# Narrow expert rounds in a two-layer transformer kernel: unsplit fp32 weights in two column tiles in place of high and low halves

## The chip, the cores and the metric

One core of one Trainium2 chip runs the whole program. The metric is the device time of one execution in microseconds, given as the median of three runs.

## The reference

Two blocks follow one another on x of 256 tokens by 1024 features, in float32. The first block has two layers; the second of them ends in a mixture of experts, and that is the part in question. The second block (attention over compressed and selected keys, retention, convolution, a 4096-wide feed-forward part) is untouched.

```
def moe_ffn(x, router_w, w1, w3, w2):
    logits = (xt @ router_w).astype(F32)
    top_v, top_i = lax.top_k(logits, TOP_K)                 # 2 of 8 experts for each token
    top_w = jax.nn.softmax(top_v, axis=-1)
    gates = jnp.sum(jax.nn.one_hot(top_i, N_EXPERTS) * top_w[..., None], axis=1)
    for e in range(N_EXPERTS):
        y = y + gates[:, e:e + 1] * swiglu(xt, w1[e], w3[e], w2[e])
# swiglu(x, w1, w3, w2) = (silu(x @ w1) * (x @ w3)) @ w2 ; w1, w3: 1024 x 3584, w2: 3584 x 1024
```

## The kernel before, in words

**Units.** All weights come through one ring of slots, loaded by SyncE in the order of use. In the expert part a unit is 128 x 2048 floats (1 MB). One expert takes 42 units: 28 for w1 and w3 (front units, `first_unit`), 14 for w2 (back units, `back_unit`). The ring has 9 slots there; `unit` on SyncE loads into a slot once TensorE has finished with the unit that held it.

**Halves.** A weight is used as two fp32r numbers: ScalarE writes the high half of a unit (`ahead`, L2049), VectorE the low half (`split`, L2660: weight minus high half), three units ahead of TensorE. A dense product is then three fp32r matmuls (`products`, L1081 to L1083: high x high, high x low, low x high), so a dense unit is 12 matmuls with 512 moving columns.

**Rounds.** Experts are sorted by their number of tokens. Eight rounds run: rounds 0, 2, 4, 6 are dense (up to 128 tokens), rounds 1, 3, 5, 7 are few (`few(r)`, up to 64 tokens). Round 2 (`LARGE`) holds up to 32 tokens beyond 128; these "thin" tokens use the unsplit weights in plain fp32, four column tiles of 32 at a time (`thin_tiles`, L1620). Further rounds stand under a condition and don't run with this input.

**A few round.** Its 64 token columns lie in the array twice, high half beside low half of the activations (`gathered_few`, 128 columns). `products_few` (L1612, L1613) multiplies these by the high and by the low weights: a few unit is 8 matmuls of 512 columns. The result has high and low contributions in different PSUM rows, so ScalarE copies it out raw (`raw_out`, L2260), TensorE turns and adds it by a matmul with a folding matrix (`turn_tile`, L1581, 8 matmuls for a 512-wide tile), ScalarE applies silu (L2288), VectorE multiplies (L3240) and the product is split in halves again (L2304, L3260). Round 3 uses transposes (L1599) and sums on VectorE (L3247) in place of the folding matmuls.

**Order.** The order is written out by hand. Step s runs the front of round s, and in between the back of round s-1 (`first_matrices`, `back_after`): two front units, one back unit. Step 0 has no back, step 8 is the back of round 7 alone (`second_matrix`). After set unit numbers come the small pieces: transposes (`turned_after`), gathers of tokens for the next round (L1503), gate rows (L1540, L1543) and scattering of the finished round (L1555, in two pieces `add_spare` on VectorE, L3226). Each engine walks the same list and waits by semaphores.

Of the kernel before, what the change touches and what calls it, by code (L numbers as in the profile page):

```python
# [52 lines left out]
EXPERT_LEAD = EXPERT_HIGHS - 1  # L53
# [143 lines left out]
class Counts:  # L197


    def __init__(self):  # L200
# [4 lines left out]
        self.raws, self.folded, self.few_turned = Tally(), Tally(), Tally()  # L205
# [21 lines left out]
ADDED_CHOOSE_AT, ADDED_GATHER_AT = 11, (13, 14, 15, 16, 20, 21, 22, 23)  # L227
# [37 lines left out]
def thin(lot):  # L265

    return lot[1] == THIN


def gather_order(r):  # L270


    return (0, 2, 4, 6, 1, 3, 5, 7) if any(map(thin, gathered_lots(r))) else tuple(range(8))


def bank_lots(r, i):


    return [lot for lot in gathered_lots(r) if i == 0 or not thin(lot)]
# [22 lines left out]
def outputs_before(r):  # L302

    return 2 * r + (1 if r > LARGE else 0)


def few_before(r):

    return sum(few(q) for q in range(r))
# [19 lines left out]

def large_units():  # L330


    stream = [unit for s in range(N_EXP + 1) for unit in step_units(s)]
    at = [n for n, (r, _) in enumerate(stream) if r == LARGE]
    assert [stream[n][1] for n in at] == list(range(MOE_UNITS))
    return at
# [16 lines left out]
def first_place(r, i):  # L353
# [4 lines left out]
    if i < PAIRED:  # L358
        pair, at = divmod(i, 2 * PAIR_UNITS)
        m, k = divmod(at, PAIR_UNITS)  # L360
        banks = [0, 1] if r == LARGE + 1 else [2 * m, 2 * m + 1]
        return [2 * pair, 2 * pair + 1], m, k, banks
    m, k = divmod(i - PAIRED, TILE_UNITS)
    return [LAST_TILE], m, k, [m if r in (LARGE - 1, LARGE + 1) else 2 * m]
# [12 lines left out]
def turned_after(r, i):  # L377
# [3 lines left out]
    if r == LARGE + 1:  # L381
        return []
    return [i // 4 - 2, i // 4 - 1] if i >= 9 and i % 8 == 1 else []


def adds_up(r):

    return r in (LARGE, LARGE + 1)


def added_after(r, i):

    if r == LARGE:
        return [i // 4] if i % 4 == 2 else []
    return [i // 4 - 2 + i % 8 - 1] if r == LARGE + 1 and i >= 9 and i % 8 in (1, 2) else []


def lows_after(r, i):

    if i < 2 or not few(r):  # L400
        return []
    if not adds_up(r):
        return turned_after(r, i - 2)
    return added_after(r, i - 2) + (added_after(r, i - 1) if i == FIRST_UNITS - 1 else [])


def gather_at(r):

    return LARGE_GATHER_AT if r == LARGE else ADDED_GATHER_AT if adds_up(r) else GATHER_AT


def choose_at(r):

    return LARGE_CHOOSE_AT if r == LARGE else ADDED_CHOOSE_AT if adds_up(r) else CHOOSE_AT + (2 if r == 0 else 0)


def tail_added_at(r):

    return TAIL_AT if r == LARGE + 1 else None


def tail_low_at(r):

    if r is None or not few(r):
        return None
    return TAIL_AT + 2


def rounds(eng, body, routed, extra, ids=False):
# [21 lines left out]
    further(0)  # L451

# [7 lines left out]
def build(nc, A, out):  # L460
    ctx = ExitStack()
    with ctx:
# [74 lines left out]
        with one:  # L537
# [31 lines left out]
            fold = sb("fold", [P, FEW], where=one)  # L569
# [9 lines left out]
        gathered_few = [params_parts[:, i * 1024:(i + 1) * 1024].rearrange("p (c n) -> p c n", n=P)  # L579
                        for i in range(2)]  # L580

        def gathered(lot):

            _, _, _, many, place = lot
            if thin(lot):
                return [thin_x]
            return gathered_many if many else [gathered_few[place][:, :, i * FEW:(i + 1) * FEW] for i in range(2)]
# [7 lines left out]
        def pairs_of(bank):  # L595

            return bank[:, :].rearrange("p (k n c) -> p k c n", c=EXPERT_ROWS, n=P)
# [8 lines left out]
        ye_high, ye_low = gparts[:, 1024:2048], gparts[:, 2048:3072]  # L606
# [6 lines left out]
        raw_few = [gbuf[:, a:a + 1024].rearrange("p (i n) -> p i n", i=2) for a in (0, 2048)]  # L613
# [15 lines left out]
        def raw_of(r, t, m):  # L629

            return thin_raw[m] if r == LARGE else raw_few[m][:, t % 2, :]

# [3140 lines left out]
```

## Time and profile before

| | us |
|---|---|
| median of 3 runs | 2295.61 (2289.98 to 2296.39) |
| the profiled execution's own time | 2291.09 |
| its span | 2289.1 |
| TensorE busy | 2240.2 (98%) |
| VectorE busy | 1821.1 (80%) |
| ScalarE busy | 1377.9 (60%) |
| mean granted TensorE clock | 0.998 |
| moved from HBM | 580 MB, 254 GB/s over the span |

The expert part lies between 428.3 and 1383 us. Busy time of TensorE counts a matmul from its start to the end of its latency, so matmuls that follow each other at 0.23 us show 0.39 us each; the pace is read from start to start. PE is TensorE's multiplication, PEld its weight load, DVE VectorE, ACT ScalarE, SP or SPq SyncE and its DMA queue. In the timeline the second number of a merged row is the time from the first start to the last end.

### The profile page before, as it was taken

The numbers are of one execution on the slowest core, as the hardware profiler recorded it, in microseconds if no ns is written. First come the engines' busy times: TensorE is split into PE (matmuls) and PEld (weight loads), VectorE is DVE, ScalarE is ACT, GpSimd is POOL, SyncE is SP. The second block draws the span as 40 slices with busy tenths as digits, with TensorE's granted clock in tenths as the row PEclk, the third lists the DMA queues.
The fourth block names the chain that finished last, engine by engine and source line by source line (L and its number), as shares of the span: only waits on it lengthen the run. The fifth ranks groups of instructions, "written<-read, shape, count | busy, mean of one in ns | idle before, by whom it ended". The sixth has DMA issues, their size and how long they took to land.

```text
span 2289.1 us, 29232 instructions
## 1 busy us (share of the span) xinstructions
PE 2240.2 (98%) x11083; PEld 1818.3 (79%) x11083; DVE 1821.1 (80%) x2362; ACT 1377.9 (60%) x1569; POOL 31.7 (1%) x44
## 2 busy tenths in 40 slices
PE   8999998999999999999999998999999999999998
PEld 6788887888866677788887876888888888888887
DVE  4965468989878898999899997999764579987555
ACT  4444444578756777787878883565454436654543
POOL 0000000000000000000000000000000000000000
PEclk9999999999999999999999999999999999999999
DMA  8366554699978999999999996545566665355563
GB/s 289 111 214 189 185 166 166 261 338 408 363 257 294 328 366 350 367 408 414 397 384 407 413 381 213 165 125 164 167 203 193 182 191 173 112 190 179 188 189 120
DMA packets 198507, 584.19 MB, mean 255 GB/s; under 512 B 17259, under 2 KB 26615, under 8 KB 183640
## 3 DMA queue, kind: packets, MB, share of 16 engines
q1 hardware_dynamic: 196060, 573.97, 71.1%
q0 software_dynamic: 1872, 6.82, 0.8%
q8 instruction: 91, 1.49, 0.3%
q10 hardware_dynamic: 428, 1.45, 0.2%
q14 instruction: 56, 0.46, 0.1%
HBM read 580.07 MB, written 2.12 MB: 254 GB/s over the span
## 4 chain that ended last, share of the span: by engine, by line
PE 85%; DVE 9%; ACT 2%; issue 2%; DMA 1%; POOL 0%; DVEq 0%; POOLq 0%; ACTq 0%; SPq 0%
PE tile L1081 20%; PE tile L1083 19%; PE tile L1082 19%; PE aux L1204 3%; DVE units_parts L2660 3%; PE tile L1612 3%; PE tile L1613 3%; PE aux L1081 2%; PE tile L1620 2%; PE aux L1083 2%; PE aux L1082 2%; PE aux L1613 1%; PE aux L1612 1%; PE aux L1581 1%; PE aux L1503 1%
## 5 line engine op out<-in xcount | busy, mean ns | idle before, releaser
L2660 DVE TENSOR_TENSOR units_parts<-units,high 128x1024 fp32r<-128x1024 f32 (+3 forms) x339 | 482.4, 1441 | 87.5 <-ACT high L2049 84.6
L1082 PE MATMUL tile<-units_parts,acts 128*128 128x512 f32 (+2 forms) x1344 | 513.7, 382 | 0.0
L2049 ACT ACTIVATE high<-units 128x1024 fp32r<-128x1024 f32 (+3 forms) x339 | 412.3, 1235 | 150.1 <-PE tile L1083 44.3
L1081 PE MATMUL tile<-high,acts 128*128 128x512 f32 (+2 forms) x1012 | 401.4, 397 | 8.2 <-DVE units_parts L2660 3.4
L1083 PE MATMUL tile<-high,acts 128*128 128x512 f32 (+2 forms) x1012 | 388.8, 384 | 0.0
L1082 PEld LDWEIGHTS tile<-units_parts,acts 128*128 128x128 f32 x1344 | 253.1, 188 | 46.5 <-issue 1.7
L1081 PEld LDWEIGHTS tile<-high,acts 128*128 128x128 f32 x1012 | 190.4, 188 | 56.8 <-issue 17.7
L1083 PEld LDWEIGHTS tile<-high,acts 128*128 128x128 f32 x1012 | 190.1, 188 | 38.5
L1082 PE MATMUL tile<-units_parts,zbuf_parts 128*128 128x512 f32 x328 | 127.6, 389 | 0.0
L1083 PE MATMUL tile<-high,zbuf_parts 128*128 128x512 f32 x256 | 99.7, 389 | 0.0
L3411 DVE SCALAR_TENSOR_TENSOR zbuf<-cbuf,taps,zbuf 128x256 f32<-128x256 f32 x240 | 99.6, 479 | 0.0
L2660 DVE TENSOR_TENSOR units_parts<-units,acts 128x2048 fp32r<-128x2048 f32 x39 | 89.2, 2287 | 12.8 <-ACT acts L2049 12.6
L2080 ACT ACTIVATE acts<-aux 128x512 fp32r<-128x512 f32 x48 | 27.3, 596 | 117.5 <-PE aux L1204 117.4
L2660 DVE TENSOR_TENSOR units_parts<-units,gbuf_parts 128x2048 fp32r<-128x2048 f32 x39 | 89.1, 2285 | 7.0 <-ACT gbuf_parts L2049 6.9
L1612 PE MATMUL tile<-high,params_parts 128*128 128x512 f32 x220 | 87.4, 397 | 1.9 <-ACT gbuf L2260 1.9
L1613 PE MATMUL tile<-units_parts,params_parts 128*128 128x512 f32 x224 | 87.5, 391 | 0.0
L2049 ACT ACTIVATE gbuf_parts<-units 128x2048 fp32r<-128x2048 f32 x39 | 74.8, 1919 | 12.3 <-PE tile L1083 8.1
L2049 ACT ACTIVATE acts<-units 128x2048 fp32r<-128x2048 f32 x39 | 74.7, 1915 | 4.2 <-PE tile L1083 2.3
L1081 PE MATMUL tile<-high,zbuf_parts 128*128 128x512 f32 x184 | 72.2, 392 | 0.0
L3699 DVE TENSOR_TENSOR gbuf<-gbuf 128x1024 f32<-128x1024 f32 x16 | 19.6, 1226 | 66.1 <-ACT gbuf L2073 66.1
L2073 ACT ACTIVATE gbuf<-tile,row_scale 128x512 f32<-128x512 f32 x36 | 24.3, 687 | 79.4 <-PE tile L1083 79.3
L1082 PEld LDWEIGHTS tile<-units_parts,zbuf_parts 128*128 128x128 f32 x328 | 61.6, 188 | 12.4
(567 smaller groups left out, 5067.6 us busy)
## 6 DMA issues: line engine op xcount, KB each, us to landing
units<-in_moe_w SPq DMA_DIRECT2D x156, 1024.0 KB, 7.9
units<-in_w_in SPq DMA_DIRECT2D x134, 512.0 KB, 4.0
units<-in_w_ff SPq DMA_DIRECT2D x128, 512.0 KB, 3.7
q_buf<-in_moe_w SPq DMA_DIRECT2D x39, 1024.0 KB, 7.6
k_buf<-in_moe_w SPq DMA_DIRECT2D x39, 1024.0 KB, 7.7
nat<-in_moe_w SPq DMA_DIRECT2D x39, 1024.0 KB, 8.0
bias<-in_moe_w SPq DMA_DIRECT2D x39, 1024.0 KB, 8.6
units<-in_ffn_w SPq DMA_DIRECT2D x48, 512.0 KB, 4.2
```

What stands on the lines that cost most here:

```text
L1081: nc.tensor.matmul(bank, lhs[0], high, start=start, stop=False)
L1082: nc.tensor.matmul(bank, lhs[0], low, start=False, stop=False)
L1083: return nc.tensor.matmul(bank, lhs[1], high, start=False, stop=stop)
L1204: mm = nc.tensor.transpose(bank[0:m, i * k:(i + 1) * k], src, ident[0:k, 0:k])
L1612: nc.tensor.matmul(bank[:, :], both, high, start=start, stop=False)
L1613: return nc.tensor.matmul(bank[:, :], both, low, start=False, stop=stop)
L1620: mm = nc.tensor.matmul(bank[at, :], rows_, of, start=start, stop=stop, tile_position=(0, c * THIN))
L2049: nc.scalar.activation(high_slot(SG[0], n) if wide_ else high_slot(SG[0], n)[:, 0:cols], halves(weights) if wide_ else weights[:, 0:cols], ...
L2073: nc.scalar.activation(dst, tiles[n % 4][:, 0:width], func, scale=scale).then_inc(SG[0].tile_evac, 1)
L2080: nc.scalar.activation(dst, aux[k % 4][0:p, 0:n * m].rearrange("p (n m) -> p n m", n=n), ACT.Copy).then_inc(SG[0].turned_high, 1)
L2660: V.tensor_tensor(low, weights, high, ALU.subtract).then_inc(SG[0].low_ready, 1)
L3411: ins = V.scalar_tensor_tensor(y_t[:, c, :], u_t[:, c, j:j + SEQ], taps[:, c, j:j + 1], y_t[:, c, :], ALU.mult, ALU.add)
```

## The change

In rounds with at most 64 tokens the weights are no longer split. `raw_unit` waits for the load alone; `few_tiles` multiplies the 64 token columns by the unsplit weights in plain fp32, output columns 0 to 511 in array columns 0 to 63, output columns 512 to 1023 in array columns 64 to 127. A few unit becomes 4 such matmuls of 512 columns (8 of 256 in the last tile). Both halves of the output lie in one PSUM bank, silu and product are taken there as in a dense round, and 4 transposes turn two 512-wide tiles; the folding matmuls, the raw copies and the second splitting go, in round 3 too. ScalarE and VectorE pass over the few rounds' units (`splits`), and look up to 4 units ahead (`led_to`). Gathers for a few round fetch whole tokens (high and rest added in the bank) instead of two halves. The few rounds' scattering takes 64 rows of the array at a time.

```
+def split_units():
+    return [n for n, (r, _) in enumerate(EXPERT_STREAM) if not few(r)]
...
+        def led_to(sig_, n):
+            m = expert_unit(sig_, n)
+            own = [of for of in split_at if of > m][:EXPERT_LEAD]
+            return n + max([1] + [of - m for of in own if of - m <= UNIT_LEAD])
...
+                    def raw_unit():
+                        n = C.unit.take()
+                        weights, _, loaded, loads = slot(S, n)
+                        pe.wait_ge(loaded, 16 * loads)
+                        return weights
+
+                    def few_tiles(bank, width, lhs, weights, start, stop):
+                        for h in range(2):
+                            mm = nc.tensor.matmul(bank[h * FEW:(h + 1) * FEW, 0:width], lhs,
+                                                  weights[:, h * width:(h + 1) * width], start=start, stop=stop,
+                                                  tile_position=(0, h * FEW))
+                        return mm
...
-                                if few(r):
-                                    mm = products_few(tiles[bank], both[:, at_k, :], high[:, row_, at], low[:, row_, at],
-                                                      start, stop)
...
+                        if few(r):
+                            width = 512 if paired else 256
+                            weights = raw_unit().rearrange("p (c n) -> p c n", c=chunks)
+                            for c in range(chunks):
+                                at_k = chunks * k + c
+                                mm = few_tiles(tiles[banks[0]], width, gathered(lots(r)[0])[0][:, at_k, :],
+                                               weights[:, c, :], at_k == 0, at_k == KC - 1)
...
-                        if few(r) and not adds_up(r):
-                            raws_of(r, t)
-                            bank = spare_bank("folded", r, t)
-                            for m in range(2):
-                                for c in range(4):
-                                    at = m * 4 * FEW + c * FEW
-                                    mm = nc.tensor.matmul(bank[:, at:at + FEW], raw_of(r, t, m)[:, c * P:(c + 1) * P],
-                                                          fold[:, :], start=True, stop=True)
...
                         if few(r):
-                            parts = [(sel_t, ye_high), (sel_t, ye_low)]
+                            rows_ = slice(h * FEW, (h + 1) * FEW)
+                            nc.tensor.matmul(bank[:, :], sel_t[rows_, b, :], ye_high[rows_, :], start=True, stop=False,
+                                             tile_position=(h * FEW, 0))
...
@@ ScalarE (ahead) and VectorE (split) @@
                     n = C.split.take()
+                    if not splits(SG[0], n):
+                        continue
...
@@ SyncE (multiplied), after the last round @@
-                sp.wait_ge(ye_ready, outputs_before(r + 1) - 1)
+                sp.wait_ge(ye_ready, outputs_before(r + 1))
```

In the instruction order a row is an operation with output and inputs, its size (output rows by moving columns for a matmul), and how often it stands in a row. The first place is TensorE in step 5 (front of round 5, back of round 4), where the first two tiles of round 5 are turned. Before:

```order
L1083 MATMUL aux1<-gbuf_parts,zbuf_parts 128x512
L1612 MATMUL tile0<-high,params_parts 128x512
L1613 MATMUL tile0<-units_parts,params_parts 128x512
L1612 MATMUL tile0<-high,params_parts 128x512
L1613 MATMUL tile0<-units_parts,params_parts 128x512
L1612 MATMUL tile1<-high,params_parts 128x512
L1613 MATMUL tile1<-units_parts,params_parts 128x512
L1612 MATMUL tile1<-high,params_parts 128x512
L1613 MATMUL tile1<-units_parts,params_parts 128x512
L1581 MATMUL aux3<-fold,gbuf 128x64 x8
L1581 MATMUL aux2<-fold,gbuf 128x64 x8
```

With the change, at the same place (L1599 is `few_tiles`, L1566 the transposes, L1073 to L1075 the dense product):

```order
L1075 MATMUL aux1<-acts,zbuf_parts 128x512
L1599 MATMUL tile0<-units,params 64x512 x4
L1566 MATMUL aux2<-consts_sb,gbuf 128x128 x4
L1599 MATMUL tile0<-units,params 64x512 x4
L1073 MATMUL aux0<-gbuf_parts,zbuf_parts 128x512
L1074 MATMUL aux0<-bias2_parts,zbuf_parts 128x512
L1075 MATMUL aux0<-gbuf_parts,zbuf_parts 128x512
```

A few unit is one group of 4, the 16 folding matmuls are 4 transposes, and the array goes from full width to 64-column tiles and back twice within these rows. The second place is TensorE in step 3 with the change, near its end, where full-width gathers (L1495, L1501), few units and thin groups (L1609, four tiles of 32 columns) meet:

```order
L1501 MATMUL aux2<-sc_parts,x_sb_parts 128x64 x2
L1599 MATMUL tile1<-nat,params 64x512 x4
L1495 MATMUL aux3<-sc_parts,x_sb_parts 128x128 x4
L1609 MATMUL tile2<-bias2,gain 32x512 x4
L1599 MATMUL tile1<-units,params 64x512 x4
L1073 MATMUL aux0<-high,zbuf_parts 128x512
```

Here the tile width changes from 32 to 64 directly, with no full-width work between. The third place is VectorE in step 5, whose low halves (L2660 before, L2624 after) dense units wait for. Before:

```order
L2660 TENSOR_TENSOR units_parts<-units,acts 128x2048
L2660 TENSOR_TENSOR units_parts<-units,gbuf_parts 128x2048
L2660 TENSOR_TENSOR units_parts<-units,high 128x2048 x2
L2660 TENSOR_TENSOR bias2_parts<-bias2,acts 128x2048
L2660 TENSOR_TENSOR q_buf_parts<-q_buf,gbuf_parts 128x2048
L3240 TENSOR_TENSOR zbuf<-zbuf,aux3 128x4x64
L3240 TENSOR_TENSOR zbuf<-zbuf,aux2 128x4x64
L2660 TENSOR_TENSOR k_buf_parts<-k_buf,high 128x2048
L2660 TENSOR_TENSOR nat_parts<-nat,high 128x2048
L2660 TENSOR_TENSOR gain_parts<-gain,acts 128x2048
L3260 TENSOR_TENSOR zbuf_parts<-zbuf,zbuf_parts 128x4x64 x2
```

With the change (L3189 adds scattered rows, L3222 multiplies silu by the second product, L3154 chooses tokens):

```order
L3189 TENSOR_TENSOR acc<-acc,aux3 128x512
L3189 TENSOR_TENSOR acc<-acc,aux2 128x512
L2624 TENSOR_TENSOR units_parts<-units,acts 128x2048
L3222 TENSOR_TENSOR gbuf<-gbuf,tile1 128x512
L2624 TENSOR_TENSOR bias2_parts<-bias2,gbuf_parts 128x2048
L2624 TENSOR_TENSOR nat_parts<-nat,high 128x2048
L2624 TENSOR_TENSOR units_parts<-units,high 128x2048
L3154 TENSOR_SCALAR sc_parts<-consts_sb,by_round 128x128 x4
```

Only the dense back units are split now; the ring's other slots go by unsplit.

## Rows read from the trace of the kernel before

**Rows 1.** Windows of steps 0 to 8: start:end, length, busy per engine, clock, DMA share, GB/s

```profile
428.30:513.10 84.80, 83.68 (x402) 69.83 (x401) 77.37 (x62) 63.07 (x53) 0.00 (x0) 1.00 0.93 341
513.10:624.50 111.40, 110.96 (x572) 90.77 (x571) 99.85 (x59) 92.95 (x85) 0.00 (x0) 1.00 1.00 390
624.50:780.20 155.70, 152.38 (x806) 104.87 (x804) 121.04 (x116) 98.37 (x93) 0.00 (x0) 1.00 0.82 285
780.20:902.40 122.20, 117.67 (x595) 85.41 (x595) 108.92 (x76) 90.20 (x85) 0.00 (x0) 1.00 0.98 360
902.40:1015.50 113.10, 113.10 (x502) 91.06 (x503) 106.52 (x65) 89.81 (x66) 0.00 (x0) 1.00 0.97 376
1015.50:1125.90 110.40, 108.39 (x540) 89.96 (x539) 102.81 (x65) 92.99 (x88) 0.00 (x0) 1.00 1.03 411
1125.90:1236.20 110.30, 110.30 (x504) 90.47 (x503) 104.11 (x63) 87.54 (x64) 0.00 (x0) 1.00 1.01 389
1236.20:1340.00 103.80, 102.16 (x496) 84.03 (x495) 97.66 (x59) 85.87 (x69) 1.64 (x3) 1.00 1.03 411
1340.00:1383.00 43.00, 38.97 (x163) 28.45 (x162) 37.04 (x26) 28.80 (x22) 0.00 (x0) 1.00 0.75 305
```

**Rows 2.** What the DMA queue itself waited for, 428.3 to 1383: total us, times, longest

```profile
SPq L878 <- PE tile L1083: 341.9, 110, 18.9
SPq L878 <- PE tile L1613: 232.3, 116, 5.0
```

**Rows 3.** DMA issues of expert weights: count, KB each, median us from issue to landing

```profile
units<-in_moe_w SPq DMA_DIRECT2D x156, 1024.0 KB, 7.9
```

**Rows 4.** Groups by line, VectorE, 428.3 to 1383: busy, mean ns, idle before and releaser

```profile
L2660 DVE TENSOR_TENSOR units_parts<-units,high 128x2048 fp32r<-128x2048 f32 x78 | 177.3, 2287 | 25.2 <-ACT high L2049 24.9
```

**Rows 5.** Timeline of TensorE, a few unit of round 5 and the folding behind it

```profile
1078.67 0.39 PE L1612 MATMUL tile<-high,params_parts 128*128 128x512 f32 x1
...
1080.26 0.39 PE L1613 MATMUL tile<-q_buf_parts,params_parts 128*128 128x512 f32 x1
1080.49 1.78 PE L1581 MATMUL aux<-fold,gbuf 128*128 128x64 f32 x15
```

**Rows 6.** Pool means in the first block, two tiles of 64 columns: timeline, then the line's durations

```profile
84.39 1.08 PE L1384 MATMUL aux<-zbuf 128*64 128x256 f32 x8
...
L1384 PE MATMUL aux<-zbuf x32: 379/379/431, 84.4 to 379.4; 128*64 128x256 f32 x32
```

**Rows 7.** Full-width plain fp32 of 512 columns (scattering): timeline, then the line's durations

```profile
1355.06 1.88 PE L1555 MATMUL aux<-gbuf,zbuf 128*128 128x512 f32 x4
...
L1555 PE MATMUL aux<-gbuf,zbuf x32: 590/592/667, 638.7 to 1362.4; 128*128 128x512 f32 x32
```

**Rows 8.** Timeline of TensorE around one thin group, full width before and behind it

```profile
642.79 0.49 PE L1599 MATMUL aux<-consts_sb,zbuf 128*128 128x128 f32 x3
643.21 1.06 PE L1620 MATMUL tile<-units,params 128*32 128x512 f32 x8
644.21 0.50 PE L1081 MATMUL tile<-high,acts 128*128 128x512 f32 x1
644.54 0.40 PE L1082 MATMUL tile<-units_parts,acts 128*128 128x512 f32 x1
```

**Rows 9.** Groups by line, the folding matmuls: count, busy, mean ns

```profile
L1581 PE MATMUL aux<-fold,gbuf 128*128 128x64 f32 x336 | 38.8, 273 | 0.0
```

**Rows 10.** Waits of TensorE, 428.3 to 1383: total us, times, longest

```profile
PE tile L1612 <- DVE units_parts L2660: 3.1, 8, 1.0
PE tile L1081 <- ACT gbuf L2260: 2.6, 1, 2.6
PE tile L1612 <- ACT gbuf L2260: 1.9, 2, 1.0
PE tile L1612 <- DVE gbuf L3273: 1.8, 1, 1.8
...
PE aux L1081 <- DVE bias_parts L2660: 1.2, 1, 1.2
```

More of the change, by code:

```diff
@@ L262, in lots, with unsplit @@
     return [(2 * FEW, CAP, column_of(r), True, 0)] + ([(4 * FEW, THIN, ROUNDS, False, 1)] if r == LARGE else [])
-def thin(lot):
-    return lot[1] == THIN
+def unsplit(lot):
+    return not lot[3]
 def gather_order(r):
-    return (0, 2, 4, 6, 1, 3, 5, 7) if any(map(thin, gathered_lots(r))) else tuple(range(8))
+    return (0, 2, 4, 6) if all(map(unsplit, gathered_lots(r))) else (0, 2, 4, 6, 1, 3, 5, 7)
 def bank_lots(r, i):
-    return [lot for lot in gathered_lots(r) if i == 0 or not thin(lot)]
+    return [lot for lot in gathered_lots(r) if i == 0 or not unsplit(lot)]
 def gathered_lots(r):
@@ L302, in outputs_before @@
 def outputs_before(r):
-    return 2 * r + (1 if r > LARGE else 0)
-def few_before(r):
-    return sum(few(q) for q in range(r))
+    return sum(1 if few(q) else 3 if q == LARGE else 2 for q in range(r))
 def column_of(r):
@@ L451, in rounds @@
     further(0)
+EXPERT_STREAM = [unit for s in range(N_EXP + 1) for unit in step_units(s)]
 def wait(eng, sem, value):
@@ L1498, in gather_bank @@
                         width = columns.stop - columns.start
[L1499 removed]
+                        both = [slice(lot[0], lot[0] + lot[1]) for lot in lots_ if unsplit(lot)]
                         for i in range(2):
@@ L1508, in gather_bank @@
                                 for b in range(TB):
-                                    mm = nc.tensor.matmul(bank[:, first:first + THIN], rest[:, b, at],
+                                    mm = nc.tensor.matmul(bank[:, first:first + own.stop - own.start], rest[:, b, at],
                                                           chosen[:, b, own], start=False, stop=(b == TB - 1))
@@ L1700, in back_unit @@
                         if k == 0:
-                            for h in range(2):
+                            for h in range(1 if few(r) else 2):
                                 take_bank(out_bank(r, h), ye_ready, out_first + h + 1)
@@ L1711, in back_unit @@
                                 chunk = EXPERT_ROWS * k + c
[L1712 to L1719 removed]
+                                mm = products(aux[h][:, :], [part[:, chunk, :] for part in hide_t],
+                                              high[:, c, at], low[:, c, at], chunk == 0, chunk == D_FFE // P - 1)
+                            if k == BACK_UNITS - 1 and h == 0:
                                 mm.then_inc(S.tile_full, 1)
@@ L2059, in used @@
                 C.unit.take(units)
-                if expert_unit(SG[0], C.unit.n - 1) >= 0:
-                    lead = EXPERT_LEAD
-                ahead(min(C.unit.n + lead, END[0]))
+                last = C.unit.n - 1
+                ahead(min(led_to(SG[0], last) + 1 if expert_unit(SG[0], last) >= 0 else C.unit.n + lead, END[0]))
             def evac(dst, closes, func=ACT.Copy, width=512, scale=1.0, also=None, units=None):
@@ L2306, in tiles_out @@
                     def tiles_out(r, i):
                         tiles_, m, _, banks = first_place(r, i)
-                        if m == 1 and not few(r):
+                        if m == 1:
                             return
@@ L3284, in first_matrices @@
                     tiles_, m, _, banks = first_place(r, i)
-                    if closes(r, i) and m == 1 and not few(r):
+                    if closes(r, i) and m == 1:
                         dve.wait_ge(S.unit_done, C.unit.n)
```

337 lines of the change are left out of this document (130 added, 207 removed).

## The prediction

> **What bounds the kernel now.** I read the windows of the expert part first, step by step, since the change touches nothing else [rows 1]. They add up to 954.7 us of the 2289. TensorE is in flight for 937.6 us of them, VectorE for 855, and HBM delivers up to 411 GB/s: three resources near their limit, so the question is which of them the steps wait for. The DMA queue's own waits settle it for the loads: SyncE stood 574 us behind TensorE alone in the two rows shown [rows 2]. It issues a load when TensorE frees a slot of the nine, and a load lands 7.9 us later [rows 3], about three units' time. So some five or six units lie landed ahead of TensorE. The weights follow TensorE, they don't lead it, although at 411 GB/s a unit of 1.049 MB costs 2.55 us and a step of 42 units 107 us, little less than steps 4 to 6 take. VectorE needs 2.29 us for each low half [rows 4], 96 us for a step of 42, and has its other work beside; TensorE waits for it and for ScalarE's copies in places, some 11 us in the larger entries [rows 10]. The path is mostly TensorE's own issue, so I price the change on TensorE, and then ask what VectorE and the loads do.
>
> **The passes.** A few unit is 8 fp32r matmuls. From the first to the last start of one are 1.59 us for 7 steps, 0.227 each [rows 5], so 1.82 us a unit, and 4 rounds of 42 units are 168. With the change it is 4 plain fp32 matmuls of 512 columns, two on either half of the array. Plain fp32 shows two records per matmul, 0.43 us apart at 512 columns ((1.88 - 0.59) / 3, [rows 7]). Whether two tiles of 64 columns run side by side is visible already: four such fp32 matmuls of 256 columns give eight records, whose first starts spread over 1.08 - 0.38 = 0.70 us [rows 6]. One after another they would spread over 7 x 0.215 = 1.5; as pairs over 3 x 0.215 = 0.65. So they pair, and a unit is four steps of 0.43, 1.72 us. 168 x (1.82 - 1.72) = **16 us less**; if the step is 0.455, nothing.
>
> **The folding.** 336 records at 0.108 apart ((1.78 - 0.27) / 14, [rows 5, 9]) go: **36 us less**. Fourteen transposes for each few round come, 56 in all at 0.11, 6 us; round 3 loses as many of its own (L1599, 7 tiles of 8). These cancel.
>
> **The edges.** The array's tile width changes between full-width and column-tiled work, and a weight load isn't pulled over such a change. The thin groups show the price. The last of three transposes starts at 642.79 + 0.49 - 0.27 = 643.01; the thin group starts at 643.21, where 643.12 would be the pace: 0.09. From there to the second dense matmul at 644.54 are 1.33 us, where two passes and one fp32r matmul make 1.09: 0.24. Together 0.33 us for one excursion [rows 8]. Before, 42 thin groups each make one. Counting in the changed order every stretch that isn't full-width, I find 23, 24, 18, 14, 21, 14, 18 and 4 in steps 1 to 8, 136 in all. 94 more at 0.33: **31 us more**. Inside these stretches 50 changes between tiles of 32 and 64 columns, or to the 64-row scattering, have no row; they lie between nothing and a full 0.33, and I take 0.15, near the 0.09 of an entry: **7.5 us more** (0 to 16).
>
> What drains at an edge is stated by the Trainium skill (TensorEngine Tiling (Array Packing), Key Properties): a change of tiling mode, not of tile alone, drains TensorE. That rule speaks against a kernel that changes modes 136 times; it names no price, the 0.33 us above is this trace's.
>
> **Gathers, scattering, end.** Round 1, 3, 5 and 7's tokens are gathered whole: 128 matmuls and 80 narrow ones in place of 160 and 16, about **2 us more** at 0.11. Few scattering keeps its count. The next block's loads now wait for all of the last output rather than its first half: **0.7 us more**, ScalarE's copy being one instead of two in turn.
>
> **Waits.** VectorE loses 168 low halves of 2.29 us, ScalarE as many high halves; VectorE falls to about half busy in the few steps. The waits on low halves and on raw copies in rows 10 (3.1, 2.6, 1.9, 1.8, 1.2) make 10.6 us, and step 8 goes at VectorE's pace (37.0 of 43.0 us busy) where TensorE needs about 3 less: **14 us less** (0 to 17). For these I name no new wait: silu and product of a few tile have the 6 us of the next units, as in dense rounds.
>
> **Sum.** -16 - 36 + 31 + 7.5 + 2 + 0.7 - 14 = -25 us, against the profiled execution's own 2291.1: 2266. The median of the runs is 4.5 above that execution, the runs spread over 6.4. I put the median after at **2267**.
>
> **Do the loads keep up?** By the same terms steps 4, 6 stay near 112, step 5 falls to 104 and step 7 to about 96. Five landed units are worth 13 us. Step 5 needs 3 of them, gets them back in step 6, step 7 needs 11, and step 8 has 14 units (36 us) for its 36. It holds, narrowly.
>
> **Rivals.**
> - *The waits stay* (12%). Other late work takes the place of the low halves, such as products that stand behind unit_done. Then only TensorE's own terms count: 2267 + 12 = 2279. For it: the few steps have closing waits in both forms. Against: VectorE is half idle.
> - *The loads become the bound* (6%). If the landed units are fewer than I think, steps 5 and 7 take 107 each: 3 + 11 us more, 2281. For it: 411 GB/s at a share of 1.03 in these steps [rows 1]. Against: the queue waits for TensorE [rows 2].
> - *Edges cost more than they give* (5%), the case on the slower side. All 144 edges added (94 + 50) stand against 61 us of gain elsewhere, so from 0.43 us each there is none. At 0.55, if a 64-column tile loads its weights later than a 32-column one or the drain of a row-tiled group is longer, 79 us stand against 61: 2311. Against: the entry into the pool means is no longer than into a thin group.
> - *Column tiles overlap only in part* (2%). Then a unit has more than four steps: at, say, 1.6 times one tile's pace in place of 2 it would be 8 x 0.43 / 1.6 = 2.15 us, and 168 x 0.43 = 72 us more, 2339. The spread of 0.70 us [rows 6] speaks against it, and so does the thin group with four tiles in 1.06 us [rows 8]. The Trainium skill (TensorE: Matmul & The Clock Gate, Measured speedup vs the span model) gives 2.38x for three column tiles, which would be such a case; the rows here don't bear it out.
>
> That the change doesn't do what it says has no room: the changed order has no folding and 168 low halves fewer.
>
> **The numbers.** The forecast case has 75%, with a range of its own from 2250 to 2278. Below it: inner changes free and edges at the 0.18 of two entries alone, 21 us less, 2246. Above: waits stay and the step is 0.44 instead of 0.43 (7 us), 2286. The range 2247 to 2286 takes these in and leaves out the two slow rivals and some of the rest. A measurement here can tell 0.3%, 7 us, from no change: below 2288.7 is faster. The forecast, the first two rivals and little else lie there: 0.89; 0.05 within, 0.06 slower.
>
> **What would show it.** Few units at 1.72 us on TensorE, with steps of 0.43; dense ones unchanged. Excursions at 0.33. L2660's successor with 168 fewer, its waits gone from TensorE's list. Steps 1, 3, 5, 7, 8 shorter by 4 to 8 us each, 4 and 6 unchanged within 2, 2 shorter by about 2. Wrong would be: steps 5 and 7 at 107 with TensorE waiting for `in_moe_w`; step 4 or 6 longer by over 4; a spacing of 0.86 between a tile's records.

## The result and the profile after

| | before | after |
|---|---|---|
| median of the runs, us | 2296.4 | 2274.4 |
| range of the runs, us | 2290.0 to 2302.7 | 2270.7 to 2280.2 |
| profiled execution, own time / span, us | 2291.1 / 2289.1 | 2274.4 / 2272.6 |
| expert part, steps 0 to 8, us | 949.8 | 930.6 |

The ratio is 0.991 with a 95% interval of 0.9883 to 0.9937: faster by 0.9%, inside the range, 7 us less gain than the forecast of 2267. Of the 16.7 us between the two profiled executions the expert part holds 19.2; the start of the part lies 2.2 later, behind work that the change does not touch.

Windows of the steps after the change, answering to [rows 1] (start:end, length, then busy time of PE, PEld, DVE, ACT and POOL, the granted clock as a share, the DMA share and GB/s):

```profile
430.50:515.40 84.90, 83.87 (x403) 69.65 (x401) 74.60 (x59) 58.61 (x47) 0.00 (x0) 1.00 0.92 338
515.40:626.40 111.00, 107.98 (x527) 56.94 (x526) 41.33 (x26) 40.34 (x42) 0.00 (x0) 0.97 1.00 394
626.40:776.60 150.20, 150.05 (x786) 87.66 (x784) 85.52 (x95) 65.58 (x68) 0.00 (x0) 1.00 0.83 288
776.60:893.60 117.00, 116.31 (x608) 58.03 (x605) 44.20 (x32) 40.88 (x42) 0.00 (x0) 1.00 0.99 377
893.60:1009.90 116.30, 116.30 (x497) 75.11 (x497) 69.41 (x44) 57.45 (x43) 0.00 (x0) 1.00 0.98 384
1009.90:1112.70 102.80, 102.80 (x505) 56.01 (x501) 43.03 (x31) 39.52 (x40) 0.00 (x0) 1.00 1.02 410
1112.70:1225.80 113.10, 113.10 (x491) 73.67 (x492) 70.81 (x44) 57.51 (x44) 0.00 (x0) 1.00 1.01 403
1225.80:1331.90 106.10, 98.55 (x456) 50.63 (x452) 37.14 (x24) 30.95 (x25) 1.64 (x3) 0.99 1.02 412
1331.90:1361.10 29.20, 29.12 (x123) 9.32 (x122) 2.75 (x4) 1.10 (x3) 0.00 (x0) 0.99 0.85 355
```

Steps 2, 3 and 5 are shorter by 5.5, 5.2 and 7.6 us. Step 1 gained 0.4 where 4 to 8 was forecast, steps 4 and 6 are longer by 3.2 and 2.8. The boundary between steps 7 and 8 is drawn a little differently here; together they took 141.9 (to the last unit at 1378.1) and take 135.3, 6.6 less where 8 to 16 was forecast. VectorE went from 109 busy to 44 in step 3, so it is no limit any more. In steps 1 and 7, PE is busy 3 and 7.5 us less than the step is long, and in step 1 the clock's mean is 0.97: those two steps have waits.

TensorE's own time, from the spacing of the matmul starts over all steps, each start charged at its form's pace. What lies up to 0.25 us above the pace is called an edge, what lies above that a wait:

| us | dense | few | thin | fold, transposes, gathers, scatter | edges | waits |
|---|---|---|---|---|---|---|
| before | 456.6 | 304.2 | 36.0 | 111.1 | 21.3 | 20.2 |
| after | 456.6 | 288.0 | 36.0 | 77.0 | 53.6 | 18.6 |
| difference | 0 | -16.2 | 0 | -34.1 | +32.3 | -1.6 |

The first four columns are counts times pace. Passes that ran at half clock, described below, are in the last two columns: some 3 us of them count as edges and some 2 as waits. The few units and the folding went as forecast. Edges grew by less than the 38.5 forecast; waits hardly fell. The timeline of TensorE in step 5 shows two few units with transposes between them and a dense unit on either side (start, length, engine, line, operands, count):

```profile
1040.71 0.39 PE L1075 MATMUL aux<-acts,zbuf_parts 128*128 128x512 f32 x1
1041.03 1.94 PE L1599 MATMUL tile<-units,params 128*64 128x512 f32 x8
1042.90 0.66 PE L1566 MATMUL aux<-consts_sb,gbuf 128*128 128x128 f32 x4
1043.49 1.94 PE L1599 MATMUL tile<-units,params 128*64 128x512 f32 x8
1045.36 0.50 PE L1073 MATMUL aux<-gbuf_parts,zbuf_parts 128*128 128x512 f32 x1
1045.69 0.40 PE L1074 MATMUL aux<-bias_parts,zbuf_parts 128*128 128x512 f32 x1
1045.93 0.39 PE L1075 MATMUL aux<-gbuf_parts,zbuf_parts 128*128 128x512 f32 x1
```

A few unit is eight records, two at a time. From 1043.49 to 1045.36 are 1.87 us: four steps of 0.43 and 0.15 for the first pair and the way out. The way in is 0.09 (0.32 from the last dense start to the first few start, where 0.227 is the pace), and the first dense matmul behind takes 0.33 instead of 0.227, another 0.10. Some 0.34 us for an excursion, and the next few dense passes stand at 0.23 to 0.24: the thin group of [rows 8] again, for a few unit.

What TensorE waited for, 430 to 1362 (us in total, times, longest), answering to [rows 10]:

```profile
PE aux L1073 <- DVE k_buf_parts L2624: 3.1, 1, 3.1
PE tile L1609 <- DMA bias<-in_moe_w: 3.0, 1, 3.0
PE aux L1073 <- DVE bias_parts L2624: 2.3, 2, 1.6
PE aux L1073 <- DVE units_parts L2624: 1.1, 1, 1.1
PE aux L1073 <- DVE nat_parts L2624: 1.1, 1, 1.1
PE aux L1495 <- DVE zbuf_parts L3197: 1.0, 1, 1.0
```

The waits for low halves (L2624, the L2660 of before) are there again, but they are others: each belongs to one of the last five dense units of step 7, and the halves are late because the load was. ScalarE (ACT), which makes the high half, waited for that load, and VectorE (DVE) followed ScalarE, here for the fourth of the five:

```profile
1315.25 1.91 ACT L2037 ACTIVATE high<-bias 128x2048 fp32r<-128x2048 f32 x1 [6.90 <-DMA bias<-in_moe_w]
1317.20 2.29 DVE L2624 TENSOR_TENSOR bias_parts<-bias,high 128x2048 fp32r<-128x2048 f32 x1 [5.93 <-ACT high L2037]
1319.63 0.47 PE L1073 MATMUL aux<-high,zbuf_parts 128*128 128x512 f32 x1 [1.55 <-DVE bias_parts L2624]
```

From the landing to the first matmul are 4.4 us, the time that the two halves take one behind the other.

The two places, in TensorE's timeline. The end of step 1:

```profile
604.00 1.95 PE L1599 MATMUL tile<-nat,params 128*64 128x256 f32 x16
605.87 0.66 PE L1566 MATMUL aux<-consts_sb,gbuf 128*128 128x128 f32 x4
609.55 1.93 PE L1609 MATMUL tile<-bias,params 128*32 128x512 f32 x8 [3.02 <-DMA bias<-in_moe_w]
611.41 3.68 PE L1599 MATMUL tile<-units,params 128*64 128x256 f32 x16
615.02 1.31 PE L1609 MATMUL tile<-q_buf,params 128*32 128x512 f32 x8
```

The thin group of round 2 waits 3.0 us for its load. Behind the wait everything is slow: the group itself takes 1.93 instead of 1.06 [rows 8], and the sixteen records of 256 columns take 3.68 where the same form took 1.95 at 604.00. That is the lower of the clock's two levels, 1.2 in place of 2.4 GHz: the granted clock is 0.50 from 608.7 to 615.6. From start to start the group takes 0.87 us more than at full clock, the unit 1.74, the next group 0.24: 2.9 us behind a wait of 3.0. The end of step 7:

```profile
1322.56 1.95 PE L1599 MATMUL tile<-q_buf,params 128*64 128x256 f32 x16
1327.62 0.50 PE L1073 MATMUL aux<-acts,zbuf_parts 128*128 128x512 f32 x1 [3.11 <-DVE k_buf_parts L2624]
...
1329.23 0.63 PE L1073 MATMUL aux<-acts,zbuf_parts 128*128 128x512 f32 x1
1329.66 0.63 PE L1074 MATMUL aux<-k_buf_parts,zbuf_parts 128*128 128x512 f32 x1
```

A wait of 3.1 us for the last dense unit, and 1.6 us into that unit the passes fall to 0.43 apart, half pace, some 1.6 us lost. Neither stretch is in the profile of before.

### The profile page after: what moved, and what is told of

Its sections match the earlier page's. It is cut to its first block, busy times and chain, and to the rows that moved or that the text cites. A ratio compares the mean times of both kernels' runs of the same rounds, so it can differ in the third digit from the quotient of the medians.

```text
span 2272.6 us, 28182 instructions
## 1 busy us (share of the span) xinstructions
PE 2225.7 (98%) x10907; PEld 1623.4 (71%) x10907; DVE 1435.7 (63%) x2135; ACT 1041.6 (46%) x1301; POOL 31.7 (1%) x44
## 4 chain that ended last, share of the span: by engine, by line
PE 92%; DVE 4%; DMA 2%; issue 1%; ACT 0%; SPq 0%; POOL 0%; POOLq 0%; ACTq 0%; DVEq 0%
PE tile L1073 21%; PE tile L1075 20%; PE tile L1074 20%; PE tile L1599 9%; PE aux L1196 3%; PE aux L1599 3%; PE aux L1073 2%; PE aux L1074 2%; PE aux L1075 2%; PE tile L1609 2%; PE aux L1907 1%; DMA k_buf<-in_moe_w 1%; PE aux L1495 1%; PE aux L1566 1%; PE aux L1550 1%
## 5 line engine op out<-in xcount | busy, mean ns | idle before, releaser
L2624 DVE TENSOR_TENSOR units_parts<-units,high 128x1024 fp32r<-128x1024 f32 (+3 forms) x299 | 392.1, 1329 | 134.7 <-ACT high L2037 129.9
L2037 ACT ACTIVATE high<-units 128x1024 fp32r<-128x1024 f32 (+3 forms) x299 | 336.2, 1145 | 167.3 <-DMA units<-in_w_in 40.0
L1073 PE MATMUL tile<-high,acts 128*128 128x512 f32 (+2 forms) x1012 | 404.9, 400 | 6.0 <-DVE units_parts L2624 3.4
L1075 PE MATMUL tile<-high,acts 128*128 128x512 f32 (+2 forms) x1012 | 390.5, 386 | 0.0
L1073 PEld LDWEIGHTS tile<-high,acts 128*128 128x128 f32 x1012 | 191.3, 189 | 61.9 <-issue 18.2
L1075 PEld LDWEIGHTS tile<-high,acts 128*128 128x128 f32 x1012 | 190.9, 189 | 39.3
L1599 PE MATMUL tile<-units,params 128*64 128x512 f32 (+1 forms) x520 | 108.7, 550 | 0.0
L1075 PE MATMUL tile<-high,zbuf_parts 128*128 128x512 f32 x256 | 99.7, 389 | 0.0
L2067 ACT ACTIVATE acts<-aux 128x512 fp32r<-128x512 f32 x48 | 27.4, 598 | 117.0 <-PE aux L1196 117.0
L1073 PE MATMUL tile<-high,zbuf_parts 128*128 128x512 f32 x184 | 72.2, 392 | 0.0
L1599 PEld LDWEIGHTS tile<-units,params 128*64 128x64 f32 x520 | 34.0, 139 | 52.4 <-issue 48.4
L1074 PEld LDWEIGHTS tile<-units_parts,zbuf_parts 128*128 128x128 f32 x328 | 61.6, 188 | 12.4
L2624 DVE TENSOR_TENSOR units_parts<-units,gbuf_parts 128x2048 fp32r<-128x2048 f32 x21 | 48.1, 2291 | 26.7 <-ACT gbuf_parts L2037 26.7
L2624 DVE TENSOR_TENSOR units_parts<-units,q_buf_parts 128x1024 fp32r<-128x1024 f32 x43 | 51.7, 1222 | 15.8 <-ACT q_buf_parts L2037 15.5
L2037 ACT ACTIVATE q_buf_parts<-units 128x1024 fp32r<-128x1024 f32 x43 | 44.8, 1062 | 33.2 <-DMA units<-in_w_ff 22.2
L2680 DVE SCALAR_TENSOR_TENSOR x_sb<-x_sb,tile 128x512 f32<-128x512 f32 x40 | 27.1, 685 | 49.7 <-PE tile L1075 49.5
```

The costliest lines, as they stand in the source:

```text
L1073: nc.tensor.matmul(bank, lhs[0], high, start=start, stop=False)
L1074: nc.tensor.matmul(bank, lhs[0], low, start=False, stop=False)
L1075: return nc.tensor.matmul(bank, lhs[1], high, start=False, stop=stop)
L1599: mm = nc.tensor.matmul(bank[h * FEW:(h + 1) * FEW, 0:width], lhs, weights[:, h * width:(h + 1) * width], start=start, stop=stop, tile_pos ...
L2037: nc.scalar.activation(high_slot(SG[0], n) if wide_ else high_slot(SG[0], n)[:, 0:cols], halves(weights) if wide_ else weights[:, 0:cols], ...
L2067: nc.scalar.activation(dst, aux[k % 4][0:p, 0:n * m].rearrange("p (n m) -> p n m", n=n), ACT.Copy).then_inc(SG[0].turned_high, 1)
```

## The experiments

Lengths in us of the steps in every kernel, from the windows of its profiled execution:

| kernel | 0 | 1 | 2 | 3 | 4 | 5 | 6 | 7+8 | all | 5 to 8 |
|---|---|---|---|---|---|---|---|---|---|---|
| before | 84.8 | 111.4 | 155.7 | 122.2 | 113.1 | 110.4 | 110.3 | 141.9 | 949.8 | 362.6 |
| changed | 84.9 | 111.0 | 150.2 | 117.0 | 116.3 | 102.8 | 113.1 | 135.3 | 930.6 | 351.2 |
| half loads | 84.8 | 105.2 | 150.2 | 116.0 | 116.3 | 102.8 | 112.9 | 125.8 | 914.0 | 341.5 |
| grouped | 84.8 | 111.3 | 148.9 | 119.1 | 113.1 | 103.6 | 109.7 | 139.3 | 929.8 | 352.6 |
| half loads, grouped | 84.8 | 103.8 | 148.8 | 116.6 | 113.2 | 101.1 | 109.8 | 123.0 | 901.1 | 333.9 |
| look-ahead 3 | 84.8 | 105.5 | 153.0 | 115.3 | 116.5 | 103.2 | 113.0 | 134.5 | 925.8 | 350.7 |
| look-ahead 3, grouped | 84.8 | 106.2 | 150.9 | 115.4 | 113.3 | 102.8 | 109.8 | 139.9 | 922.9 | 352.4 |
| early backs | 84.7 | 109.7 | 150.2 | 117.6 | 116.3 | 103.3 | 113.1 | 134.5 | 929.5 | 350.8 |
| all three | 84.7 | 107.7 | 150.8 | 115.5 | 113.2 | 102.9 | 109.8 | 138.4 | 923.0 | 351.1 |

The part before step 0 is touched by none of them, and still its end lies anywhere from 427 to 438 us in these executions. So the lengths of the steps tell apart what the medians, a few us of scatter each, can't.

**Half loads.** Few rounds load half of every unit and both column tiles multiply that half:

```diff
+                part_ = 2 if few(r) else 1
-                    unit(S, lambda v: v.rearrange("p (c n) -> p c n", c=2),
-                         w[r0:r0 + 2 * P, pair * D:(pair + 1) * D]...
+                    unit(S, lambda v: v.rearrange("p (c n) -> p c n", c=2)[:, :, 0:D // part_],
+                         w[r0:r0 + 2 * P, pair * D:pair * D + D // part_]...
...
-                                                  weights[:, h * width:(h + 1) * width], start=start, stop=stop,
+                                                  weights[:, 0:width], start=start, stop=stop,
```

> Left out: of every unit of the four few rounds only half the columns are loaded, and both column tiles multiply that half. TensorE's instructions stay the same in number, shape and order; only 168 loads carry 0.5 MB instead of 1. Theory (loads): the waits at the ends of step 1 (3.2 us) and step 7 (8.4 us) and the half clock behind them go, steps 1 and 7 are 5 and 9 us shorter, steps 4 and 6 keep their 116 and 113 within 1; the whole about 2274 - 14 = 2260. Rival (the halves' chain): ScalarE and VectorE are late there whatever has landed; under 3 us are gained, 2272. Second rival (steps 4 to 8, whose 182 units took 2.57 us each, follow the loads throughout and not only at the end): steps 4 and 6 become shorter too, over 20 us in all, below 2252.

Measured: median 2259.6, ratio to before 0.9845 (0.9819 to 0.9872). Windows of steps 1, 6, 7 and 8:

```profile
519.90:625.10 105.20, 105.20 (x528) 56.27 (x527) 41.16 (x26) 39.67 (x42) 0.00 (x0) 1.00 0.86 291
...
1110.40:1223.30 112.90, 112.90 (x489) 73.55 (x489) 69.11 (x43) 57.29 (x43) 0.00 (x0) 1.00 0.89 309
1223.30:1317.50 94.20, 94.20 (x445) 47.87 (x442) 36.83 (x24) 29.65 (x24) 1.64 (x3) 1.00 0.90 308
1317.50:1349.10 31.60, 31.60 (x134) 11.25 (x134) 3.13 (x5) 1.76 (x3) 0.00 (x0) 1.00 0.45 150
```

Step 1 is 5.8 us shorter and steps 7 and 8 together 9.5; steps 2, 4, 5 and 6 stay as they were. PE is busy the whole of every step shown, the clock is 1.00, and of the list of TensorE's waits one entry of 1.0 us remains for the whole part. By the spacing the waits are 5.4 us, 14.8 less than before the change. The 5.8 us of step 1 are its wait of 3.0 and the 2.9 at half clock. So the 14 us of waits that were to go did go, and the loads put 13 others in their place. The second rival, loads that pace steps 4 to 6 too, falls for this kernel.

**Grouped.** Second-matrix units come two at a time behind every four first-matrix units:

```diff
-        return [BACK_UNITS - 1]
-    return [i // 2 - 1] if i >= 2 and i % 2 == 0 else []
+        return [BACK_UNITS - 2, BACK_UNITS - 1]
+    return [i // 2 - 2, i // 2 - 1] if i >= 4 and i % 4 == 0 else []
```

> Second-matrix units stand in pairs behind every four first-matrix units, instead of one behind every two, in steps 1, 2 and 4 to 7. Counted in the order, TensorE leaves full width 29 times less and makes 6 fewer inner mode changes. Theory (an excursion costs 0.33 us): TensorE's edges fall from 48.6 to about 39 us; steps 4 and 6 give 1.5 us each, step 7 gives none of it (its loads are late already), the whole 2274 - 7 = 2267. Rival (the 31 us of edges are something else, such as the first matmul behind a change of operands): edges stay within 2 us of 48.6, no gain. Rival (two dense units in a row find the second one's halves late): edges fall, waits for the low halves grow by as much, no gain.

Measured: median 2271.5, ratio 0.9892 (0.9872 to 0.9913), not to be told from the changed kernel's 0.991. Edges fell by 10.7 us for 29 excursions less, 0.37 each with their inner changes, and waits grew by 10.2. Steps 4 to 8:

```profile
899.90:1013.00 113.10, 113.10 (x497) 76.26 (x497) 67.36 (x43) 54.81 (x42) 0.00 (x0) 1.00 0.99 389
1013.00:1116.60 103.60, 101.63 (x505) 56.78 (x502) 42.71 (x30) 39.79 (x40) 0.00 (x0) 1.00 1.02 410
1116.60:1226.30 109.70, 109.70 (x489) 74.74 (x489) 69.18 (x44) 56.16 (x44) 0.00 (x0) 1.00 1.03 411
1226.30:1323.60 97.30, 89.88 (x432) 46.80 (x428) 32.85 (x21) 26.97 (x21) 1.64 (x3) 1.00 1.02 411
1323.60:1365.60 42.00, 37.11 (x146) 15.66 (x146) 7.67 (x7) 6.34 (x7) 0.00 (x0) 0.92 0.87 359
```

Steps 4 and 6 gain 3.2 and 3.4 us, twice what I expected of them (the records show 7 excursions in each instead of 14, so 0.46 and 0.49 apiece, with the somewhat slower passes behind each), and steps 3, 5 and 7 with 8 give back 2.1, 0.8 and 4.0. In steps 6 and 7 HBM delivers 411 GB/s: the loads have become the pace.

**Half loads and grouped together.** The two edits above.

> Left out: half the columns of the few rounds' loads, as in the half loads run; and second-matrix units stand in pairs. With full loads the pairs saved 8.8 us of edges and gained 0.5. Theory (the loads took that gain back): with half the loads it stays gained, the expert part 914.0 - 9 = 905, the whole 2250, steps 4 and 6 3 us shorter, 5 and 7 1.5. Rival (the pairs make their own waits, for halves or for the output banks): the waits grow here as well and the expert part stays above 911.

Measured: median 2247.4, ratio 0.9785 (0.9755 to 0.9814); expert part 901.1, which is 12.9 us below half loads alone, waits 5.7 us as there. The rival of waits that the pairs make themselves falls: with the loads out of the way the gain of the pairs stays. It is larger than the 9 I expected; 29 excursions for 12.9 us make 0.44 each, inner changes and the slower first passes included.

**One tile.** Both output halves of a few unit go to the same column tile:

```diff
-                            mm = nc.tensor.matmul(bank[h * FEW:(h + 1) * FEW, 0:width], lhs,
-                                                  weights[:, h * width:(h + 1) * width], start=start, stop=stop,
-                                                  tile_position=(0, h * FEW))
+                            mm = nc.tensor.matmul(bank[0:FEW, 0:width], lhs,
+                                                  weights[:, h * width:(h + 1) * width], start=start and h == 0,
+                                                  stop=stop and h == 1, tile_position=(0, 0))
```

> Both halves of the output columns of a few unit are multiplied in the same column tile (columns 0 to 63 of the array), so that they can't run beside each other; the second half's result is added to the first's. Theory (two column tiles overlap in full, which is what makes plain fp32 as cheap as the three fp32r products of 128 columns): a few unit takes eight steps of 0.43, 3.44 us in place of 1.72; 168 x 1.72 = 289 us more, less some 9 us of waits that end with the loads' lateness, 2274 + 280 = 2554. If the overlap were partial, the difference would be under 200 us.

Measured: 2544.1 in its one run. Two few units in TensorE's timeline, beside the two of the changed kernel above:

```profile
1148.03 3.60 PE L1599 MATMUL tile<-nat,params 128*64 128x512 f32 x8
1151.46 3.60 PE L1599 MATMUL tile<-gain,params 128*64 128x512 f32 x8
```

From start to start 3.43 us, twice 1.72, with the same eight records. The few units take 576.4 us in all instead of 288.0: two tiles of 64 columns overlap in full. The waits by spacing are 3.5 us, so at this pace the loads are never late. The time is 10 us below the 2554 expected, since I had taken off 9 us of waits and the waits and half-clock passes that went are some 18.

The 2.38x for three column tiles that the Trainium skill gives (TensorE: Matmul & The Clock Gate, Measured speedup vs the span model) is no guide for these shapes; two tiles measure 2.00x here.

**Look-ahead 3.** Halves of dense units are made, and thin groups run, at most three units ahead, where the change had raised this to four:

```diff
-EXPERT_LEAD, UNIT_LEAD = EXPERT_HIGHS - 1, EXPERT_HIGHS
+EXPERT_LEAD, UNIT_LEAD = EXPERT_HIGHS - 1, EXPERT_HIGHS - 1
```

> The halves of a dense unit are made, and the thin groups run, at most three units ahead of the unit that TensorE is at, where the changed kernel allows four. Theory (the loads fall behind in the few steps 1 and 7 until fewer units lie landed than the look-ahead asks for): some 5 units were landed at the ends of steps 1 and 7, and TensorE waited there 5.1 and 8.4 us. One unit less asked for is worth 2.55 us to each stretch, and more in step 1, where a 3.2 us wait was followed by half clock: step 1 shorter by 4 to 6 us (from 111.1), steps 7 and 8 together by 2.5 to 4 (from 135.1), the others within 1; the expert part 930.3 - 8 = 922, the whole about 2266. Rival (the third unit ahead is too late for ScalarE and VectorE, so that the change needed four): new waits for low halves in the few steps, 14 dense units a step with 0.5 us or more each, the whole at or above 2274.

Measured: median 2269.1, ratio 0.9879 (0.9855 to 0.9902). Steps 1, 7 and 8:

```profile
523.10:628.60 105.50, 104.08 (x519) 56.21 (x519) 42.88 (x27) 39.31 (x40) 0.00 (x0) 1.00 1.03 407
...
1229.60:1328.30 98.70, 94.30 (x444) 47.71 (x440) 35.60 (x22) 30.98 (x25) 1.64 (x3) 1.00 1.03 411
1328.30:1364.10 35.80, 32.13 (x134) 11.32 (x134) 5.38 (x6) 2.46 (x4) 0.00 (x0) 1.00 0.91 376
```

Step 1 came out as the theory had it: 5.5 us shorter, one wait of 1.6 left, clock 1.00. Steps 7 and 8 did not: 0.8 shorter instead of 2.5 to 4, the same 8.3 us of waits. Step 2 lost 2.8. By the records TensorE leaves full width 11 times more in step 2 and makes 10 inner changes fewer, which is most of that loss. No new waits for low halves, so the rival falls; but the theory was wrong for step 7. A shorter look-ahead helped where a thin group asked four units ahead, at the end of step 1. In step 7 ScalarE begins a half at the moment the load lands in both kernels, so the look-ahead isn't what holds it. The 0.8 us are even less than the 1.6 of half-clock passes that this run lacks there.

A kernel with the thin groups alone held at three units was also written; in its order the engines come to wait for one another in a circle, so there is no time for it. What the thin groups and what the halves contributed to step 1 is therefore not measured apart.

**Look-ahead 3 and grouped.**

> Three units of look-ahead and second-matrix units in pairs together. Theory (edges cost TensorE 0.3 us each, but steps 5 to 8 go at the pace of the loads, 2.55 us a unit): edges 40 us as in the grouped run; of its 10.2 us of new waits the shorter look-ahead takes back what it takes back in the ungrouped kernel, about 8; the expert part about 921, the whole 2265, within 2 us of the run with look-ahead three alone. Rival (the two gains add up because the loads were only asked for too early): expert part 913, the whole 2257.

Measured: median 2270.4, ratio 0.9879 (0.9853 to 0.9905), expert part 922.9. That is near the 921 expected, for another reason: against grouped alone all of it came from steps 1 and 3, and steps 7 and 8 wait 14.6 us, 1 more than grouped alone.

**Early backs.** In step 7 the dense units come singly behind the few units 2 to 15, and only few units follow:

```diff
+    if s == N_EXP - 1:
+        return [i - 2] if 2 <= i < BACK_UNITS + 2 else []
```

> Only step 7 is changed: the 14 dense second-matrix units of round 6 stand one behind each of the few units 2 to 15, instead of one behind every second one up to the end; behind them only few units are left, which need no halves. Theory (from step 5 on the loads run at 2.55 us a unit and can't be hurried, but the dense unit that closes step 7 holds TensorE until its load and its two halves are there, so that some 7 landed few units, 12 us of work, are left when the last load lands): the same loads, the last landing at the same distance from the start of step 5, and two to four units left behind it: steps 7 and 8 together shorter by 5 to 9 us (from 135.1), waits of step 7 for halves gone or small, the expert part about 923, the whole about 2267. Rival (the floor is the loads alone, whatever the order): steps 7 and 8 stay within 2 us of 135.1. Rival (dense units one behind every few unit come faster than ScalarE and VectorE make halves): waits for halves early in step 7, longer than before.

Measured: median 2273.8, ratio 0.9908 (0.9886 to 0.9929); steps 7 and 8 134.5 us, 0.8 shorter. The waits of TensorE (L1601 is the few matmul here), 427 to 1358:

```profile
PE tile L1601 <- DMA units<-in_moe_w: 3.7, 7, 1.0
PE tile L1611 <- DMA bias<-in_moe_w: 2.9, 1, 2.9
PE tile L1601 <- DMA q_buf<-in_moe_w: 1.7, 1, 1.7
```

The waits for halves are gone and as many for the loads themselves stand in their place, 0.3 to 1.8 us each, at most of the few units from the end of step 7 on. I had counted seven landed units idle at the end; they weren't landed in full. The first rival, that the loads are the floor whatever the order, is what happened.

**All three**, with the dense units of step 7 in pairs, and a twin with them singly.

> Look-ahead of three, second-matrix units in pairs, and in step 7 in pairs behind the few units 2, 4 to 14. Theory: step 1 at 106 (look-ahead), steps 4 and 6 at 113 and 110 (edges), and of the 139.8 us of steps 7 and 8 in the run with the first two alone 8 to 12 are gained, since that kernel waited 14.3 us there for halves of late dense units: expert part about 913, the whole about 2260. Rival (the loads are the floor whatever the order): no better than 2270.

> As the run before, but the dense units of step 7 stand singly behind the few units 2 to 15: 14 excursions there in place of 7, which cost TensorE 3 us. Theory (step 7 goes at the pace of the loads, not of TensorE): the same time within 1.5 us, 913 for the expert part. Rival (once the order is mended TensorE is the bound again): 3 us longer.

Measured: medians 2266.4 and 2267.1, ratios 0.9873 (0.985 to 0.9896) and 0.9877 (0.9853 to 0.99), expert parts 923.0 and 924.5. Not the 913 expected: early backs again gave nothing over look-ahead and pairs. The twin with single units makes 5 more excursions in step 7 by the records, and steps 7 and 8 are not longer for it (138.0), as it must be where the loads set the pace. Both medians lie 7 to 8 us below the changed kernel's. The intervals overlap, so of these versions I claim only that steps 1, 3, 4 and 6 are shorter in the profile.

## Why the prediction was nearly right

**The floor.** The last column of the table is the main finding. The changed kernel and six others with full loads (one tile aside, which is slower than its loads) differ in order, in look-ahead and there by some 6 us in edges, and from the start of step 5 to the last unit they take 350.7 to 352.6 us (the twin with single dense units, 350.9). Only fewer bytes shorten it: 341.5 with half the few loads, 333.9 with pairs as well, where TensorE is the bound again and its edges count. The landings show why: in the changed kernel, grouped, both look-ahead runs, early backs and all three the last expert unit lands 348.5 to 349.2 us behind the start of step 5, with 134 to 136 units to land from there, one every 2.57 to 2.61 us. The prediction had all the pieces: 2.55 us a unit, 107 a step, 13 us landed ahead. For steps 5 to 8 they make 140 x 2.55 - 13 = 344 us of loads against its 104 + 112 + 96 + 36 = 348 for TensorE: 4 us of slack, no more than one dense unit's halves take behind the landing.

The Trainium skill has the HBM side bind a load at some 358 GB/s a core, a stack's 716 divided by its two cores (DMA: Bandwidth & Descriptors, Where 436 GB/s comes from). Only one core is at work here, and the windows show 410 to 412; the measurement decides.

Point by point:

- *Passes, 16 us less.* 16.2. Four steps of 0.43 a unit, the two tiles side by side; the one tile run confirms it at 2.00x.
- *Folding, transposes, gathers: 34 less.* 34.1. (The 32 gathers more, at 0.11, are 3.5 us and not the 2 in the sum.)
- *Edges, 31 and 7.5 more.* Right, and the starts in the traces show it change by change. In the half loads run, where nothing in the part is at half clock, they sum to 52.6 us against 14.4 before: 38.2 more. Each of the 136 excursions costs 0.34 (0.09 in, 0.05 at the first narrow pair, 0.10 out, 0.10 at the first full-width start), each of the 50 inner changes 0.14. Such an inner change, from 32 to 64 columns, is at the end of the group in the first row here, 0.99 us from start to start where its two passes are 0.86:

```profile
871.39 1.06 PE L1609 MATMUL tile<-bias,gain 128*32 128x512 f32 x8
872.38 1.94 PE L1599 MATMUL tile<-units,params 128*64 128x512 f32 x8
```

  The table's column of edges grew by 32.3 only, because it holds more than mode changes. The fp32r starts of the few units before lay some 7 ns above the pace, 8.6 us in all, and went with them; 3 us of half-clock passes came. In steps 4 and 6, with 14 excursions each, none before and no inner change, the column grew by 5.2 and 5.8, 0.37 and 0.41 apiece.
- *Waits, 14 less.* **This is the step that failed**: 1.6 less. "For these I name no new wait" looked at VectorE and ScalarE, which are indeed no longer late on their own account: the half loads run has 14.8 us less of waits than before.
- *"It holds, narrowly".* The same mistake, seen from the loads. It counted the units ahead as 13 us to be used up before anyone waits. A thin group asks for its unit up to four ahead, and a dense unit must have landed 4.4 us before TensorE comes to it, so only what is landed beyond that is a reserve. And it began with step 5: step 1 ran dry at its end, cost a wait of 3.0 us and 2.9 at half clock, and was not in the account.
- *The rival "the loads become the bound"*, given 6%, is half of what happened: it named steps 5 and 7 and 14 us. Step 5 used up its reserve without a wait; step 7 waited 8.4 us. The rival "the waits stay", given 12%, had a nearer number than the forecast (2279), but late work of VectorE as its cause, and half loads rules that out.
- *Steps.* 3 and 5 shorter by 5.2 and 7.6, as said; 7 with 8 by 6.6, not 8 to 16; 1 by 0.4, not 4 to 8; 4 and 6 longer by 3.2 and 2.8 where I had allowed 2; 2 shorter by 5.5 where I had said 2. Part of that is 3 us of waits that step 2 had before, for a product (1.8) and a sum (1.6) of VectorE.

In numbers: the forecast for the profiled execution was 2291.1 - 25 = 2266; add 12.4 us of waits that did not go, take off 6.2 of edges that did not come, and add the 2.2 in front of the part: 2274.5, where 2274.4 was measured. Half of the miss was made good by luck. The 6.2 are no error of the edge term, which came out as priced: they are mostly the 8.6 us above the pace that the passes term had not counted. Without them the time would have been near the rivals' 2279 and 2281, still inside the range.

## What to carry to other kernels

Before a change makes one engine faster, add up the bytes that the faster stretch asks for in its shorter time, stage by stage, and count as reserve only what is landed beyond the need of whoever asks first, work on the unit between landing and use included. When a queue waits for an engine 574 us in all, it can still be without slack in the one step that the change shortens. And test a suspected floor by taking bytes away, not by reordering: the reorderings here moved it by 2 us at most, and one run with a quarter of the bytes left out settled it.

## What the runs showed of the hardware

- A mode change on TensorE costs 0.09 us on the way in, 0.15 for the first narrow pair and the way out, 0.10 at the first full-width matmul behind; a change between tiles of 32 and 64 columns costs 0.14. Taking 29 excursions away gave 0.37 to 0.44 each, by the two pairs of runs.
- Short waits for loads were followed by the lower clock level, both at the end of step 1 (a group of 1.93 instead of 1.06, a unit of 3.68 instead of 1.95) and at the end of step 7 (passes 0.43 apart instead of 0.23). So a load stall can cost more than its own length: in step 1, 3.0 us of wait brought 2.9 us of slow passes with it.
- The length of the wait alone doesn't tell whether the clock falls. All three fell to 0.50 behind a wait of 2.1 us (first row), while in look-ahead 3 the same unit of step 7 came after 3.1 us (second row) with the clock at 1.00, and in the kernel before a wait of 2.6 us left it at 1.00 too:

```profile
609.00 1.93 PE L1611 MATMUL tile<-bias,params 128*32 128x512 f32 x8 [2.14 <-DMA bias<-in_moe_w]
...
1331.38 0.50 PE L1073 MATMUL aux<-acts,zbuf_parts 128*128 128x512 f32 x1 [3.09 <-DVE k_buf_parts L2624]
```

- One core's loads run at 410 to 412 GB/s in steps 5 and 7 of the changed, the grouped, the look-ahead 3 and the all three kernel, whatever the order of TensorE's work.
